# Pool, two attentions, output, gate/up and down projection of a two-layer block on one NeuronCore: six stages become one block by token groups

## The reference

```
h = rmsnorm(x); p = h @ w_in                      # 2560 features: u, dq, dk, dv, sq, sk, sv
a = pool_mixer(u)                                 # trailing means over 2, 4, 8, 16 tokens, 64x64 maps
b = rmsnorm((softmax(q1 k1') - lam softmax(q2 k2')) v)    # 4 heads, causal
c = rmsnorm(A v), A[t,s] = beta[t,s] * prod_{s<j<t} (1 - beta[t,j])   # 4 heads of 64, s < t
x = x + concat(a, b, c) @ w_out
h = rmsnorm(x)
x = x + (silu(h @ w_gate) * (h @ w_up)) @ w_down  # 2816 hidden features
return rmsnorm(x)
```

## Time and profile before

| | |
|---|---|
| median of 3 runs | 4464.51 us (4460.39 to 4464.7) |
| the profiled execution | 4460.61 us, of which the span is 4458.9 us |
| mean granted clock of TensorE over the span | 0.936 of 2.4 GHz |
| PE / DVE / ACT / POOL busy | 90% / 44% / 36% / 6% |

### The profile page before, as it was taken

One profiled execution on the slowest core, in us unless ns is written; L12 is line 12 of the kernel. 1 busy time (PEld: TensorE's weight loads), 2 busy tenths in 40 slices (PEclk: granted clock), 3 DMA queues, 4 the chain that ended last, 5 costly groups with the idle time before them and its releaser, 6 DMA issues. The chain is left out here.

```text
span 4458.9 us, 53760 instructions
## 1 busy us (share of the span) xinstructions
PE 4022.7 (90%) x19636; PEld 3305.0 (74%) x19636; DVE 1946.4 (44%) x2791; ACT 1588.1 (36%) x2925; POOL 254.9 (6%) x390
## 2 busy tenths in 40 slices
PE   7999999999999948878869797979999999989998
PEld 6887877778878727656658685868888888877776
DVE  3666667564454146656647672221111111024443
ACT  3334343343334225445446563431111111134432
POOL 1011111132200000000000000000000000000000
PEclk9999999999999959779779898989999999999999
DMA  5544544544444320000010005441111111044454
GB/s 169 189 161 137 175 160 148 173 134 134 147 170 160 122 93 1 38 38 10 0 66 1 11 1 171 155 142 52 42 52 42 52 42 52 28 135 171 167 174 139
DMA packets 245098, 452.06 MB, mean 101 GB/s; under 512 B 28080, under 2 KB 131504, under 8 KB 237488
## 3 DMA queue, kind: packets, MB, share of 16 engines
q1 hardware_dynamic: 227872, 393.12, 26.9%
q10 hardware_dynamic: 17040, 56.63, 3.2%
HBM read 325.96 MB, written 123.73 MB: 101 GB/s over the span
## 5 line engine op out<-in xcount | busy, mean ns | idle before, releaser
L1675 PE MATMUL fr_bank<-fr_x_hi,fr_w_hi 128*128 128x512 f32 x1792 | 725.1, 405 | 15.1 <-DVE fr_w_lo L1905 9.8
L1677 PE MATMUL fr_bank<-fr_x_hi,fr_w_lo 128*128 128x512 f32 x1792 | 704.3, 393 | 0.0
L1676 PE MATMUL fr_bank<-fr_x_lo,fr_w_hi 128*128 128x512 f32 x1792 | 703.7, 393 | 0.0
L401 PE MATMUL ff_acc<-ff_x_hi,ff_w_hi 128*128 128x512 f32 x1344 | 530.4, 395 | 0.9 <-DVE ff_w_lo L204 0.9
L402 PE MATMUL ff_acc<-ff_x_lo,ff_w_hi 128*128 128x512 f32 x1344 | 530.3, 395 | 0.0
L403 PE MATMUL ff_acc<-ff_x_hi,ff_w_lo 128*128 128x512 f32 x1344 | 530.3, 395 | 0.0
L1905 DVE TENSOR_TENSOR fr_w_lo<-fr_w_in,fr_w_hi 128x1024 fp32r<-128x1024 f32 x224 | 274.0, 1223 | 346.7 <-ACT fr_w_hi L1792 346.3
L1675 PEld LDWEIGHTS fr_bank<-fr_x_hi,fr_w_hi 128*128 128x128 f32 x1792 | 340.9, 190 | 83.6 <-DVE fr_w_lo L1905 10.2
L1677 PEld LDWEIGHTS fr_bank<-fr_x_hi,fr_w_lo 128*128 128x128 f32 x1792 | 339.7, 190 | 72.9
L1676 PEld LDWEIGHTS fr_bank<-fr_x_lo,fr_w_hi 128*128 128x128 f32 x1792 | 340.8, 190 | 64.5 <-issue 1.0
L1807 ACT ACTIVATE fr_res<-fr_bank 128x512 f32<-128x512 f32 x192 | 114.5, 596 | 637.7 <-PE fr_bank L1677 637.7
(11 more groups left out here) (272 smaller groups left out, 6342.4 us busy)
## 6 DMA issues: line engine op xcount, KB each, us to landing
fr_w_in<-in_w_in SPq DMA_DIRECT2D x192, 512.0 KB, 4.1
m_w_in<-in_w_down SPq DMA_DIRECT2D x88, 512.0 KB, 3.5
h1T<-fr_res SPq DMA_DIRECT2D x112, 256.0 KB, 2.9
ffT<-ff_res ACTq DMA_DIRECT2D x22, 1024.0 KB, 3.8
m_a_in<-ffT SPq DMA_DIRECT2D x88, 256.0 KB, 3.6
p2T<-fr_res SPq DMA_DIRECT2D x80, 256.0 KB, 2.4
fr_w_in<-y1C SPq DMA_DIRECT2D x32, 512.0 KB, 3.7
ff_w_in<-in_w_gate SPq DMA_DIRECT2D x22, 512.0 KB, 3.6
```

The source lines that it names most:

```text
L401: pe.matmul(a[:, :], w_hi[:, n, k, :], hi[:, k, t], start=k == 0, stop=False)
L1675: pe.matmul(to[:, :], w_hi[slot][:, k, :], x_hi[x % 2][:, k, :], start=k == 0, stop=False)
L1676: pe.matmul(to[:, :], w_hi[slot][:, k, :], x_lo[x % 2][:, k, :], start=False, stop=False)
L1677: m = pe.matmul(to[:, :], w_lo[slot][:, k, :], x_hi[x % 2][:, k, :], start=False, stop=k == KB - 1)
```

## The change

`front` keeps its order and gets more results. A `p2` job of kind "qk" (48 of them) now leaves two results, hi from ScalarE and lo from VectorE (one subtraction of 128x512), each stored. A job of kind "v" (24) is turned by four transposes on TensorE (`turn_v`) and copied by VectorE. Result slots go from 3 to 4.

The six later stages become one function `back`. It has four token groups g of 512 tokens. A group has 76 jobs: 8 of `m2`, then in three chunks of 8, 8 and 6 hidden blocks the pairs `gate` and `up` followed by 8 jobs `m3`. Their steps number 64 + 352 + 176 = 592 in a group, each with three matmuls of 128x512: 7104 matmuls in all, as many as before. Hidden features stay on the chip. Attention has 128 units, 32 in a group (16 "df", 16 "sb"), each 128 queries of group g against g + 1 segments of keys. The pool and the attention of group 0 stand ahead of the first job; those of group g + 1 are spread evenly over the jobs of group g; the jobs of group 3 have none between them.

```diff
+def attention_order(units, g):
+    mine = [u for u in range(len(units)) if units[u][0] == g]
+    order = [("pool", g, 0), ("pool", g, 1), ("pool", g, 2), ("keys", units[mine[0]][:2]), ("query", mine[0])]
+    segs = g + 1
+    for u in mine + [mine[-1] + 1, mine[-1] + 2]:
+        now, old, older = u in mine, u - 1 in mine, u - 2 in mine
+        new_block = now and (u == mine[0] or units[u][:2] != units[u - 1][:2])
+        if new_block and u != mine[0]:
+            order += [("pause",)] * (2 * g)
+        if u + 1 in mine:
+            order.append(("query", u + 1))
+        diff = now and units[u][1] < 4
+        first = [("scores", u, 0, j) for j in range(segs)] if diff else []
+        rest = [("scores", u, 1, j) for j in range(segs)] if diff else [("scores", u, 0, j) for j in range(segs)] if now else []
+        turns = []
+        if old:
+            if units[u - 1][1] < 4:
+                turns.append(("combine", u - 1))
+            turns += [("turn", u - 1, 0)]
+            for j in range(segs):
+                if j + 1 < segs:
+                    turns.append(("turn", u - 1, j + 1))
+                turns.append(("product", u - 1, j))
+        if older:
+            order.append(("result", u - 2, 1))
+        for n in range(max(len(first), len(turns))):
+            order += first[n:n + 1] + turns[n:n + 1]
+        if old:
+            order.append(("result", u - 1, 0))
+        if new_block:
+            order.append(("values", units[u][:2]))
+        order += rest
+        if now:
+            order.append(("weigh", u))
...
+def back_order(jobs, units):
...
+            if t < 3:
+                spread([("norm", g * 4 + t, 0), ("norm", g * 4 + t, 1)], at_job[base + 5 + t] + 2, at_job[base + 5 + t] + 8)
+            else:
+                ahead[base + 5 + t] += [("norm", g * 4 + t, 0), ("norm", g * 4 + t, 1)]
...
+            spread(attention_order(units, g + 1), at_job[base] + 2, at_job[base + per - 4])
...
+            def weigh(u):                                   # VectorE
...
+                if kind_of(u) == "df":
+                    dve.tensor_reduce(low[:, u % 2, :], ..., AX.X, ALU.min).then_inc(low_ready, 1)
+                    return
+                me.done(dve.memset(other(u)[:, w:w + 1], 1.0))
+                flip = other(u)[:, 0:w][:, ::-1]
+                me.done(dve.tensor_tensor_scan(flip, flip, zero..., 1.0, ALU.mult, ALU.add))
+                me.wait()
+                dve.tensor_tensor(weights(u)[:, 0:w], weights(u)[:, 0:w], other(u)[:, 1:w + 1], ALU.mult).then_inc(weights_ready, 1)
...
+                elif kind == "weigh" and units[of[0]][1] < 4:   # ScalarE: both maps of a df unit, one Exp each
+                    act.wait_ge(low_ready, df_to[u] + 1)
+                    for r, tile in enumerate((weights(u), other(u))):
+                        m = act.activation(tile[:, 0:width(u)], ..., ACT.Exp, scale=-1.0, bias=low[...], accum_out=total[...])
...
+                elif kind == "result" and of[1] == 0:            # GpSimd: (mean square + eps) ** -0.5
...
+            act.activation(tmp[p % 2][:, :], bank[...], ACT.Tanh, scale=0.5)   # gate: silu by way of Tanh
```

More of the change, by code:

```diff
@@ L1324, in front_order @@
                 slots[at // 3][at % 3].append(("ln", pair * 8 + t, n))
+    for j, job in enumerate(jobs[:-1]):
+        if out_kind(*job) == "v":
+            slots[j + 1][0].append(("turn_v", j))
     order = []
@@ L1349, in front @@
     first_of = {x: j for j, x in reversed(list(enumerate(operand)))}
-    by_act = [stage_ != "m1" for stage_, _, _ in jobs]
-    act_count, dve_count = [0], [0]
-    for x in by_act:
-        act_count.append(act_count[-1] + x)
-        dve_count.append(dve_count[-1] + (not x))
+    kinds = [out_kind(*job) for job in jobs]
+    act_count, m1_count, qk_count, v_count = ([0] for _ in range(4))
+    result_at, results, stores = [], [], [[0] * RES]
+    for j, x in enumerate(kinds):
+        act_count.append(act_count[-1] + (x != "m1"))
+        m1_count.append(m1_count[-1] + (x == "m1"))
+        qk_count.append(qk_count[-1] + (x == "qk"))
+        v_count.append(v_count[-1] + (x == "v"))
+        result_at.append(len(results))
+        results += {"m1": [], "plain": [True], "qk": [True, True], "v": [False, True]}[x]
+        stores.append([sum(results[slot::RES]) for slot in range(RES)])
     LN_OPERANDS = {6: 0, 7: 1, 10: 2, 11: 3}
@@ L1770, in norm_unit, with turn_v @@
                     m.then_inc(h_turned, 1)
+            def turn_v(j):
+                pe.wait_ge(act_out, act_count[j + 1])
+                for t in range(4):
+                    m = pe.transpose(bank[j % BANKS][:, t * P:(t + 1) * P], res[result_at[j] % RES][:, t * P:(t + 1) * P], ident[:, :])
+                m.then_inc(v_turned_out, 1)
             for kind, *of in order:
-                if kind == "begin":
+                if kind == "begin" and of[0] < J:
                     begin(*of)
@@ L1896, in _ @@
                     norm_unit(*of)
-            evacuate(J - 1)
         @block.vector
@@ L1912, in begin @@
             def begin(j):
-                if j and not by_act[j - 1]:
+                if 1 <= j <= J and kinds[j - 1] == "m1":
                     _, n, t = jobs[j - 1]
@@ new lines, with back_jobs @@
+POOL_WINDOWS = (2, 4, 8, 16)
+LAM_INIT = 0.8 - 0.6 * math.exp(-0.3 * 0)
+RMS_EPS = 1e-6
+MASKED = -1e30
+HD = P // 2
+SCALE = HD ** -0.5
+FB = 22
+CHUNKS = ((0, 8), (8, 16), (16, 22))
+def back_jobs():
+    jobs = []
+    for g in range(NTG):
+        jobs += [("m2", g, n, g * 4 + t) for n in range(2) for t in range(4)]
+        for c, (f0, f1) in enumerate(CHUNKS):
+            jobs += [(stage_, g, c, f) for f in range(f0, f1) for stage_ in ("gate", "up")]
+            jobs += [("m3", g, c, n) for n in range(KB)]
+    return jobs
@@ new lines, in back_units @@
+def back_units():
+    units = []
+    for g in range(NTG):
+        for b in range(6):
+            for r in range(1 if b < 4 else 2):
+                units += [(g, b, r, g * 4 + t) for t in range(4)]
+    return units
+def attention_order(units, g):
[32 more added lines that the diff above has]
+            order.append(("weigh", u))
+            if u + 1 in mine and units[u + 1][:2] != units[u][:2]:
+                order.append(("keys", units[u + 1][:2]))
+    return order
```

1815 lines of the change are left out of this document (769 added, 1046 removed).

## The result

The changed kernel takes **5013.45 us** (median of 4 runs, 5005.55 to 5013.58) against 4462.45 us before on the same chip: ratio 1.1235, 95% interval 1.1215 to 1.1255. The direction was forecast, the size was not: 5013 lies above the range (4390 to 4880), 273 us over the 4740.

A forecast was written before the change was run, and what follows sets the result against it. TensorE's work plus its waits bound the kernel. Start of groups 1879 + 1612 + 617 + 70 + 40, norm, pool and keys 134, chains 283, clock 75, tail 24 gave 4734, hence 4740 us; range 4390 to 4880.

The forecast's parts named there:

- norm and pool: TensorE's waits in the groups for norm tiles and pool sums: 80 and 34 us, both with clock.
- Front and lonely group 0: `front` ends at 1578 us, group 0's uncovered attention units take 242 us, and the groups begin at 1879.
- Last group, tail: The last group, without attention, takes near 430 us; four tiles behind the last matmul add 24 us.
- Chain waits: In groups 1 to 3 TensorE waits for attention chains: sb 208 us, df 75, together 283; bounds 90 and 400.
- Row changes: Attention entries between contraction steps cost 0.09 us per turn, product or result, half for scores: 70 us.
- Clock: Reduced TensorE clock behind about 44 long chain waits, 1.7 us lost each: 75 us; bounds 0 and 120.
- Rival 1: In the groups, entry spacing covers the chains, a quarter of waits (123 us) left: 4371 us; chance 0.27.
- Rival 2: The gates' Tanh needs its own table, two loads per gate, 169 us on ScalarE: 4825 us; chance 0.08.
- Rival 3: Border gain and chain loss cancel, waits 217 us, no change; chance 0.05 including what lies between.

The follow-up runs named there:

- whole-unit run: All edits together with longer sb pauses (4569.52 us), plus a whole unit of stagger in groups 0 to 2, four score buffers instead of three: 4530.99 us.
- short scan: Changed kernel with scan and product of an sb unit over 128 columns only, other weights left unscaled: 4783.33 us.
- pauses: Changed kernel with empty order-list entries ahead of the sb and df results and behind the combine: 4836.77 us.
- segments: Changed kernel with sb scores issued from last segment to first, each segment scanned from where the one before ended: 4922.58 us.
- late result: Changed kernel with the df result of unit u - 2 placed behind its round's scores, turns and products in groups 1 to 3: 4971.3 us.
- full rows: Changed kernel with all score matmuls over 128 rows instead of 64: 4840.61 us; the same edit together with the pauses: 4647.45 us.
- throwaway matmuls: Changed kernel with extra unread bf16 matmuls of 384 columns (8, 18, 28 a unit) ahead of the sb result waits: 4968.88 us.
- last version: Changed kernel with zero-padded 128-row scores, segmented scans, late df result, pauses, deeper stagger, and pool, keys, query and combine moved: 4435.3 us, 0.9935 of the kernel before.

## Why the prediction was wrong, point by point

I take its sum apart into what TensorE does and what it stands. It had 1879 + busy 2426 (1612 + 617 + 70 + 40, clock 75, and 12 of clock in norm and pool, 1.7 for each of seven waits) + idle 405 (283, and 134 less those 12) + tail 24 = 4734. The changed kernel has 1880 + 2675 + 439 + 18 = 5012, counted from the first `m2` matmul to the last matmul of a job (the windows above begin 10 us later, 6 of them busy).

- **Front and lonely group 0: right in sum, in part by luck.** 1880 for 1879. The df units took 9.6 us each, not 8.3 (the sb units 6.8, as forecast), some 20 us more in all; `front` ended 6 us sooner than forecast, and 11 us, not 24, lie between the last result and `m2`. The whole-unit run shows that 58 us of this head were the stagger.
- **Last group, tail: right.** 425 for 430 and 18 for 24 us.
- **Chain waits: right in mechanism and size.** Idle time is 34 us over the forecast. The sb chain is shown by the short scan (230 us less), by the pauses (sb waits 205 to 73) and by the segments (124). The df wait was placed at the turn behind the combine; it came at the result ahead of it, 93 us for 75. About a quarter of that was its place in the list, shown by the late result; why VectorE is late for the rest was read from timelines only (norm and write-outs stand ahead of the scale).
- **Row changes: the first failed step.** "For turns, products and results I take 0.09, for scores half." The scores' share was 20 us; 421 passages at 0.33 to 0.37 are 139 to 156. (By its own counts the term leaves out the 96 results, 9 us more.) The rows that it used show a unit of 128 rows between steps, and the score matmuls of the old attention stand among their own kind. No row of before has 64 rows between 128. It should have been bounded, and was halved instead. Shown by full rows, in two settings, and by the weight loads, which begin with their matmul at a change of rows and a matmul ahead elsewhere.
- **Clock: the second failed step.** "1.7 us lost" for "about 44 of the waits" was 75 us. Low spells number 76: the granted clock is low behind all 52 waits of 3.6 us and more, but also behind 9 of the 11 from 3.0 to 3.6 us, 10 of the 17 from 2 to 3 and 5 of the 19 from 1 to 2. A spell lasts 5.7 us on average and costs 2.6. That is 196 us, against 87 with norm and pool. The earlier trace rows show one wait with a shorter spell behind it than the mean here (0.61 over 2 us and 0.77 over 4); taking that one for all was the error, and the bound of 120 rested on nothing wider. The throwaway matmuls bear out the rate roughly, 42 counted and 53 found in the stretches, on a quarter of the term. The rule of the Trainium skill that the prediction named for this (TensorE: Matmul & The Clock Gate, "HAM oscillation": an array that waits once in every tile pays for a cold start every time) is borne out, and more dearly than I let it be.

The two failed steps are 119 to 136 and 109 us short, 228 to 245 together, against 249 us of missing busy time; 34 us of waits and 5 less of the rest make the 278 between the span and the forecast for it.

Rival 1 (spacing covers the chains) was false in the changed kernel: 439 us of idle time and 196 of clock, where it had 123 for both. The last version comes nearer to it: 224 us of idle time and 52 of clock, at 4435 us. Order and segmented scans alone are not enough, since with 64 rows the same list takes 4558, more than the kernel before. Rival 2 (Tanh with a table of its own) is out: `back` has eight table loads in all (L1516, L1540 and L1520), those at the borders of df and sb. Rival 3 did not occur.

Open is why the first group's weights, the write-outs and the results still make TensorE wait in the last version, and how much of the clock term belongs to waits under 3 us.

## What to carry to other kernels

When two streams of work are woven on one in-order engine, count three prices for each entry: the wait for its chain, the clock behind that wait, and the change of shape between neighbours; the last is paid where nothing waits and no list of waits shows it. Price the shape change from a row with that very neighbourhood, and if there is none, bound it. A slow weave doesn't condemn weaving: here the same work in one piece was slower still. Order (stagger, pauses, entries moved to when their input is ready) together with segmented scans took 456 us out, and zero-padded operands 122 more.

## What the runs showed of the hardware

- A change between 64-row and 128-row matmuls holds the array about 0.1 us longer on both sides of the change: 0.33, 0.33, 0.32, 0.34 instead of 0.23. The weight load of the first matmul behind the change begins with that matmul, not 0.23 ahead of it (496 of 496 places at full clock). Padding 64 rows with zeros to 128 costs nothing by the row (0.23 to 0.24 in both shapes) and removes this: 122 us in the last version, and 173 from taking all 128 rows in the changed kernel.
- The array's low level of 1.2 GHz lasted 5.7 us on average, most of it behind waits of 2 to 9 us, and filling waits with throwaway bf16 matmuls kept the higher level in the waits it covered (76 low spells to 48).
- A scan on VectorE can be cut in segments that start from an element of the one before, at a small loss: 160 scans took 175.7 us in the last version, 64 took 155.0 in the changed kernel.
